# Six modulation pieces in each of seven differential heads instead of eight in each of five

## The reference

```python
def adaln_params(cond, mod_w, mod_b):
    m = jax.nn.silu(cond) @ mod_w + mod_b          # mod_w: (1024, 6144) per layer
    return jnp.split(m[:, None, :], N_MOD, axis=-1)

def layer(x, cond, l, rope, ctx_kv):
    sh_a, sc_a, g_a, sh_f, sc_f, g_f = adaln_params(cond, mod_w[l], mod_b[l])
    o, k, v = token_mixer(modulate(x, norm_attn[l], sh_a, sc_a), l, rope, ctx_kv)
    x = x + g_a * o
    f = conv_ffn(modulate(x, norm_ffn[l], sh_f, sc_f), w_up[l], conv_w[l], conv_b[l], w_down[l])
    return x + g_f * f, k, v
```

## Time and profile before

| | us |
|---|---|
| median of 3 runs (lowest, highest) | 3609.38 (3599.21, 3609.42) |
| the profiled execution's own time | 3618.67 |
| its span, first to last instruction | 3616.9 |
| mean granted TensorE clock | 0.964 |
| TensorE busy | 3342.2 (92%) |
| VectorE, ScalarE, GpSimd busy | 1868.7, 1185.8, 942.6 |
| 40 loads of `wr<-mod_w`, 512 KB each, median to landing | 4.8 |

### The profile page before, as it was taken

The page is one execution under the profiler, slowest core; times in us unless marked ns, Lnnn a source line. Parts: engine busy times, 40 slices in busy tenths (PEclk is TensorE's granted clock), DMA queues, the critical chain, the costliest instruction groups (busy, mean ns, idle before and its releaser), DMA issues. The chain is left out here.

```text
span 3616.9 us, 51583 instructions
## 1 busy us (share of the span) xinstructions
PE 3342.2 (92%) x20797; PEld 3084.3 (85%) x20797; DVE 1868.7 (52%) x2655; ACT 1185.8 (33%) x2106; POOL 942.6 (26%) x726
## 2 busy tenths in 40 slices
PE   5898898998889999999988999999798999999997
PEld 4777777887789999999988777777598999999996
DVE  4555555555155554555545555565416545555454
ACT  3334344444232222122223555555413121222111
POOL 1122112222233322223233121221133322332221
PEclk8999999998899999999999999999899999999998
DMA  6333343113211111111112111101231111111101
GB/s 240 108 107 113 112 125 116 51 40 121 87 42 47 41 53 35 41 37 39 54 38 78 38 30 26 35 23 35 97 99 58 42 36 41 41 37 56 35 29 59
DMA packets 206659, 229.78 MB, mean 64 GB/s; under 512 B 30564, under 2 KB 173533, under 8 KB 205341
## 3 DMA queue, kind: packets, MB, share of 16 engines
q1 hardware_dynamic: 186973, 162.69, 14.8%
q10 hardware_dynamic: 11664, 42.47, 3.5%
q0 software_dynamic: 7856, 22.29, 1.7%
HBM read 181.79 MB, written 31.98 MB: 59 GB/s over the span
## 5 line engine op out<-in xcount | busy, mean ns | idle before, releaser
L205 PE MATMUL psum<-Hh,wh 128*128 128x384 f32 x3360 | 1142.2, 340 | 52.6 <-ACT Hh L377 14.7
L206 PE MATMUL psum<-Hh,wl 128*128 128x384 f32 x3360 | 1131.0, 337 | 0.0
L207 PE MATMUL psum<-Hl,wh 128*128 128x384 f32 x3360 | 1130.9, 337 | 0.0
L286 DVE SCALAR_TENSOR_TENSOR x<-psum,mod,x 128x384 f32<-128x384 f32 (+2 forms) x768 | 377.4, 514 | 684.6 <-PE psum L207 643.2
L205 PEld LDWEIGHTS psum<-Hh,wh 128*128 128x128 f32 x3360 | 636.6, 189 | 63.3 <-issue 35.5
L206 PEld LDWEIGHTS psum<-Hh,wl 128*128 128x128 f32 x3360 | 636.8, 190 | 0.0
L207 PEld LDWEIGHTS psum<-Hl,wh 128*128 128x128 f32 x3360 | 636.5, 189 | 0.0
L816 POOL TENSOR_TENSOR wl<-wr,wh 128x1024 fp32r<-128x1024 f32 x88 | 219.8, 2498 | 986.6 <-ACT wh L735 986.6
L766 ACT ACTIVATE ff_u<-psum 128x768 f32<-128x768 f32 x88 | 71.6, 814 | 1109.2 <-PE psum L207 1109.2
L205 PE MATMUL psum<-ff_ah,ff_dh 128*128 128x384 f32 x1056 | 365.1, 346 | 29.4 <-POOL ff_al L838 20.7
L964 DVE SCALAR_TENSOR_TENSOR ff_c<-ff_u,par,ff_c 128x1153 f32<-128x1153 f32 x176 | 377.4, 2144 | 15.8 <-DVE ff_c L961 5.2
(11 more groups left out here) (217 smaller groups left out, 4267.8 us busy)
## 6 DMA issues: line engine op xcount, KB each, us to landing
wr<-w_up SPq DMA_DIRECT2D x88, 512.0 KB, 3.9
ff_dr<-w_down SPq DMA_DIRECT2D x22, 1024.0 KB, 6.1
da_mw<-mod_w ACTq DMA_DIRECT2D x40, 512.0 KB, 3.9
wr<-mod_w ACTq DMA_DIRECT2D x40, 512.0 KB, 4.8
wr<-w_qkv_diff SPq DMA_DIRECT2D x24, 512.0 KB, 19.2
x<-x_save SPq DMA_DIRECT2D x16, 576.0 KB, 7.5
in_mw<-mod_w SPq DMA_DIRECT2D x8, 1024.0 KB, 12.2
Hh<-oh_save SPq DMA_DIRECT2D x14, 576.0 KB, 9.8
```

What stands on the lines that cost most here:

```text
L205: pe.matmul(out, w_hi, m_hi, start=start, stop=False)
L206: pe.matmul(out, w_lo, m_hi, start=False, stop=False)
L207: return pe.matmul(out, w_hi, m_lo, start=False, stop=stop)
L286: last = dve.scalar_tensor_tensor(g.x[:, m, lo:hi], g.PS[:, bank, lo - n * NB:hi - n * NB], g.mod[:, gate + m, cond:cond + 1], g.x[:, m, l ...
```

## The change

The 40 pieces are numbered through (m = 0 to 39) and put into the list `SLOTS` of (head, step): six in each of heads 0 to 6, at steps 1, 3, 4, 5, 7 and 8, until 40 are placed (heads 0 to 5 have six, head 6 has four, at steps 1, 3, 4 and 5). Slice 1's sum is thus complete after head 1's second piece, and so on. `("MT", i)` stands in front of the piece that begins the next slice, in the same step: head 1 step 4, head 2 step 7, head 4 step 1, head 5 step 4; the last one stands alone in head 6 step 7. TensorE does both at the front of the step, ahead of the scores, and VectorE's bias addition moves to the same place in its order. The request for the next load follows each piece as before. Where the piece before lies in the head before, a wait for the last two uses of that head takes the place of the wait for the piece.

```diff
--- before.py
+++ after.py
@@ -1204,6 +1204,16 @@
         " ck_in cv_in ko_out v_out r_d y_out sub soft y_split wo_in0 wo_in1 wo_hi wo_lo o_in", reused=True)
     free = {WORK: b.free0, WORK + 1: b.free1}
     SLICES = 5
+    SLOTS = [(h, s) for h in range(HEADS - 1) for s in (1, 3, 4, 5, 7, 8)]
+    PIECE = {at: m for m, at in enumerate(SLOTS[:SLICES * KC])}
+
+    def slice_uses(h, s):
+
+        m = SLOTS.index((h, s)) if (h, s) in SLOTS else None
+        if m is None or m > SLICES * KC:
+            return []
+        return [("MT", m // KC - 1)] * (m > 0 and m % KC == 0) + [("M", m)] * (m < SLICES * KC)
+
     mw = [b.mw[:, 0, :], b.mw[:, 1, :]] + [g.wr[:, 1, 4 * j:4 * j + 4, :].rearrange("p k n -> p (k n)") for j in range(2)]
     PROJ = [None, ("k", 1), ("k", 2), ("q", 0), ("q", 1), ("q", 2), ("v", 0), ("v", 1), ("v", 2)]
     PV_AT, ST_AT, BC_AT = {2: [0], 4: [1], 6: [2], 8: [3], 9: [4]}, {3: [0], 5: [1], 7: [2], 9: [3, 4]}, {4: [0], 6: [1], 8: [2], 9: [3, 4]}
@@ -1220,7 +1230,7 @@
         tiles = [("T", s - 1, i) for i in range(len(groups_of(s - 1)))]
         if s == STEPS - 1:
             last = tiles + [("PV", 4), ("ST", 3), ("ST", 4)] + [("W+",)] * ahead2 + [("BC", 3), ("BC", 4)]
-            return [("MT",)] * (h < SLICES) + last
+            return last
         proj = [("W",) + PROJ[s]] if ahead else []
         u = proj + tiles if s == STEPS - 2 else tiles + proj
         u += [("PV", p) for p in PV_AT.get(s, [])]
@@ -1228,7 +1238,7 @@
         if ahead and s in (2, 3):
             u += [("ck",) if s == 2 else ("ko",)]
         u += [("BC", p) for p in BC_AT.get(s, [])]
-        return [("M", s - 1)] * (h < SLICES) + u
+        return slice_uses(h, s) + u
 
     AHEAD = {("W", "k", 0): 0, ("W", "q", 0): 2, ("W", "k", 1): 1, ("W", "q", 1): 3}
     FIRST = [("W", "k", 2), ("ck",), ("ko",), ("W", "q", 2), ("W", "v", 0), ("W", "v", 1), ("W", "v", 2), ("W+",)]
@@ -1397,9 +1407,10 @@
                     copy_out(ring, use, b.ck[:, :], P)
 
             def next_slice(ring, h, s):
-                if ("M", s - 1) in step_uses(h.index, s) and (h.index, s) != (SLICES - 1, STEPS - 2):
-                    act.wait_ge(b.full, ring.done(("M", s - 1)))
-                    load_slice(act, h.index + (s == STEPS - 2), s % KC)
+                m = PIECE.get((h.index, s))
+                if m is not None and m + 1 < len(PIECE):
+                    act.wait_ge(b.full, ring.done(("M", m)))
+                    load_slice(act, (m + 1) // KC, (m + 1) % KC)
 
             def first(ring):
                 load_slice(act, 0, 0)
@@ -1510,15 +1521,18 @@
                 if what == "W+":
                     return project(ring, use, after(h, 2 if ring.head is not None else 1), "k", 0)
                 if what == "M":
-                    k = use[1]
+                    k = use[1] % KC
                     ring.wait_free(pe, free, use)
-                    pe.wait_ge(b.mw_in, 32 * (KC * h.index + k + 1))
+                    pe.wait_ge(b.mw_in, 32 * use[1] + 32)
                     for j in range(4):
                         last = pe.matmul(PS[32 * j:32 * j + 32, bank, :], g.sc[:, k, :], mw[j], start=True, stop=True)
                     last.then_inc(b.full, 1)
                     return
                 if what == "MT":
-                    ring.wait_read(pe, free, ("M", KC - 1))
+                    if ("M", KC * use[1] + KC - 1) in ring.names:
+                        ring.wait_read(pe, free, ("M", KC * use[1] + KC - 1))
+                    else:
+                        ring.wait_earlier_read(pe, free)
                     ring.wait_free(pe, free, use)
                     for k in range(4):
                         last = pe.transpose(PS[:, bank, k * P:(k + 1) * P], b.acc[:, k * P:(k + 1) * P], g.ident[:, :])
@@ -1591,13 +1605,12 @@
             def body(h, ring, ahead, ahead2):
                 for s in range(STEPS):
                     uses = step_uses(h.index, s)
-                    for use in uses[:1]:
-                        if use[0] == "M":
-                            do(ring, h, use)
+                    for use in slice_uses(h.index, s):
+                        do(ring, h, use)
                     if 0 < s < TILES:
                         scores_by_rows(h, s)
                     for use in uses:
-                        if use[0] == "M":
+                        if use[0] in ("M", "MT"):
                             continue
                         if ahead and use == ("PV", 4):
                             scores_by_rows(after(h, 1), 0)
@@ -1652,15 +1665,19 @@
                 dve.scalar_tensor_tensor(b.y[:, (h.odd + p) % 2, 0:n], b.o[:, p % 2, 0:n], b.wsub[:, :], PS[:, ring.bank(use), 0:n],
                                          ALU.mult, ALU.mult).then_inc(free[ring.bank(use)], 1)
 
-            def accumulate(ring, h, k):
-
-                use = ("M", k)
+            def accumulate(ring, use):
+
                 dve.wait_ge(b.full, ring.done(use))
                 src = PS[:, ring.bank(use), :]
-                if k == 0:
+                if use[0] == "MT":
+                    done = add_mod_bias(g, dve, use[1] + 1, src)
+                elif use[1] % KC == 0:
                     done = dve.tensor_copy(b.acc[:, :], src)
                 else:
-                    ring.wait_read(dve, free, ("M", k - 1))
+                    if ("M", use[1] - 1) in ring.names:
+                        ring.wait_read(dve, free, ("M", use[1] - 1))
+                    else:
+                        ring.wait_earlier_read(dve, free)
                     done = dve.tensor_tensor(b.acc[:, :], b.acc[:, :], src, ALU.add)
                 done.then_inc(free[ring.bank(use)], 1)
 
@@ -1676,8 +1693,8 @@
                 for s in range(TILES):
                     for p in BC_AT.get(s - 1, []):
                         normalise(ring, h, p)
-                    if ("M", s - 1) in step_uses(h.index, s):
-                        accumulate(ring, h, s - 1)
+                    for use in slice_uses(h.index, s):
+                        accumulate(ring, use)
                     if s:
                         maxima(h, s)
                     if ahead and s in K_ROPE:
@@ -1690,9 +1707,6 @@
                     combine(h, s)
                     for p in ST_AT.get(s, []):
                         mean_square(ring, p)
-                if h.index < SLICES:
-                    dve.wait_ge(b.full, ring.done(("MT",)))
-                    add_mod_bias(g, dve, h.index + 1, PS[:, ring.bank(("MT",)), :]).then_inc(free[ring.bank(("MT",))], 1)
                 for p in BC_AT[TILES - 1]:
                     normalise(ring, h, p)
                 for p in ST_AT[TILES]:
```

## The result

The changed kernel takes 3579.28 us (median of four runs, 3571.60 to 3582.87), the kernel before 3606.07 us in the same series. The ratio is 0.9925, with a 95% interval of 0.9902 to 0.9949. A second series gave 3579.08 us against 3601.19, ratio 0.9937 (0.9922 to 0.9951). The forecast was 3578; the gain by the medians is 22 to 27 us where 31 was said.

A forecast was written before the change was run, and what follows sets the result against it. TensorE, busy 92%, bounds the kernel; only its idle time and slow stretches can be won. 23.0 + 7.5 + 7.7 - 4.2 - 2.8 = 31.2 us off the 3609.38 us median gives 3578 us, range 3563 to 3597.

The forecast's parts named there:

- Load waits: Heads 0 to 4, steps 2 and 6: TensorE's waits for slice weights go, 23.0 of 26.7 us, 17.67 at step 6.
- Slow clock: Behind step 6's wait, piece and scores return to full clock: 1.5 us in each of five heads, 7.5 us.
- a sign of being wrong: Waits above 1 us at step 4 or 8, ScalarE waiting for weights, or head 2 well above 100 us.
- Pieces back in heads 5 and 6: The ten moved pieces bring new waits, mostly for PSUM banks, in heads 5 and 6: 4.2 us added.
- The transposes: The sum's transposes leave the front of step 9, saving 7.7 us, and cost 2.8 us in the new place.
- Head 0's slow stretch: Head 0 at 220 to 230 us, clock 0.66: left as is; with its slow start about 3 us, either way.
- The cover to watch: Heads 5 and 6: weight loads get slices beside them; landing taken as 18.7 to 19.7 us, tightest with 2 us spare.
- A: Rival: slices stretch weight loads past the 2 us spare, ScalarE stands at the weight conversion; 3581 to 3595 us; 8%.
- C: Rival: loads in steps 3 to 5 and 7 to 8 wait as much as steps 2 and 6 did; 3609 us; 4%.
- D: Rival, slower: weight load beside slice moves to steps 3 or 7, and 13 places pay wait and clock; 3643 us; 3%.
- B: Rival: the wait moves, as another link holds the following step, and half of the 31 us is lost; 3594 us; 6%.

The follow-up runs named there:

- experiment 2: Changed kernel with seven pieces a head, at steps 1, 2, 3, 4, 5, 7, 8 (only step 6 left out); ratio 0.9943 against the kernel before.
- experiment 4: Kernel before, no piece moved, SyncE loading the k weights behind the swap of the queries instead of ahead of it; ratio 0.9947 against the kernel before.
- experiment 6: Changed kernel with the pieces of steps 3 and 7 requested one step ahead instead of two; ratio 0.9938 against the kernel before.
- experiment 5: Changed kernel once more, no edit; ratio 0.9937 against the kernel before.
- experiment 8: Kernel before, eight pieces a head, with request ahead of ScalarE's copies and sum's transposes in front of the next slice; 3573.15 us, ratio 0.9906.
- experiment 3: Changed kernel with seven pieces a head, at steps 1, 3, 4, 5, 6, 7, 8 (only step 2 left out); ratio 0.9980 against the kernel before.

## Why the prediction was right, by its own steps

1. *Load waits (23.0 us of 26.7 to go).* Right: 26.7 - 4.9 = 21.8 us went, with seven waits of 0.44 to 1.55 left where I counted seven summing to 4.2. Right as well that step 6 is the bulk (experiment 2). The reason was half right. More room between request and use does end the waits, but the numbers for it were off: I took the distance from piece to piece, 9 to 13 us before and some 20 after. What counts is the time from ScalarE's issue to the use. Behind a short step it is about 4.2 us before TensorE stands waiting (experiment 4, step 6 of head 2: 4.84 - 0.65), behind a long one 8.5, with two steps 16 to 17. A slice takes 4.8 us in the median, so a short step leaves nothing over. Experiment 6 shows that 8.5 us are enough. What was missing is why step 6 was so much worse than its likes: a weight load issued just ahead of its slice (experiment 4). The prediction had noticed that company and used it only for rivals. In the changed kernel the company is still there (in head 5 the slice requested in step 5 landed after 9.2 us); the piece is just not due before 16.6.

2. *Slow clock (7.5 us).* Right in kind: the clock is 1.00 in heads 1 to 6 of the changed kernel, and likewise in experiment 4, where only the wait was taken away. In size too: between the first trace of before and experiment 4, heads 1 to 4 together became 17.4 us shorter (436.3 to 418.9) and their load waits only 11.0 (20.0 to 9.0); the 6.4 between are 1.6 a head, where 1.5 was said. Two statements failed. The waits left were not all under 1 us: one was 1.55 us at step 8 of head 4, which the prediction had named as a sign of being wrong; it comes with a long issue on ScalarE's queue (below) and cost no slow clock. And in the traces of experiments 5 and 6, waits of 1.60 and 1.72 us at the same place were followed by a slow stretch. With experiment 2, where 2.46 us were not, the runs leave open what besides the wait decides it. Behind the 1.60 us, experiment 5:

```profile
597.76:601.00 3.24, 3.24 (x16) 1.65 (x17) 1.99 (x7) 0.34 (x2) 2.11 (x4) 0.55 0.14 21
```

3. *Pieces back in heads 5 and 6 (4.2 us).* Measured 3.3 us as the cost of spreading, between two kernels without load waits, so 0.49 of the 4.2 could not show there. In head 2 the waits at steps 3 to 5 are those predicted.

4. *The transposes (7.7 out, 2.8 in).* The old place is confirmed (1.55 against 1.54). The new one costs 0.71 instead of 0.56, so the term is 4.2 us, not 4.9.

5. *Head 0's slow stretch* was left as it is, and went: it is absent in the changed kernel and also in the second trace of the kernel before, so it is no effect of the change. Of the 33.2 us, 21.8 of waits, 7.5 to 8 of clock and 4.2 of MT, less 3.3 for the spreading, leave 2.5 to 3. I put them down to this stretch, but that is not shown: head 0 of the second trace of the kernel before has no such stretch and load waits shorter by 2.9 us, and yet is only 1.5 us shorter (115.50 against 117.00).

*The cover to watch was read wrongly.* The prediction says that a weight load takes 18.7 to 19.7 us to land over the whole kernel, beside slices or not the earlier trace rows. These are the times of two loads out of 24, both of the input phase (issued at 10.3 and 11.0 us, L491). For the 22 loads of L1277, all those of the heads among them, the trace has no landing. Asked for L491 alone the view gives the same three numbers, asked for L1277 alone it gives none. The two groups come first below; then a window of 4 us shows the packets of the load issued at 683.12 in head 5, with no slice near. Below them the same for the one issued at 394.68, 1.5 us ahead of a slice, and from experiment 4 a window that begins 4 us after the issue at 392.36 (396.4 to 400.9):

```profile
L1277 SPq DMA_DIRECT2D wr<-w_qkv_diff x22: 378/384/582, 82.3 to 773.7; - x22
L491 SPq DMA_DIRECT2D wr<-w_qkv_diff x2: 681/4629/8577, 10.3 to 11.0; - x2
...
DMA packets 1184, 0.59 MB, mean 147 GB/s; under 512 B 32, under 2 KB 1184, under 8 KB 1184
...
DMA packets 1243, 0.83 MB, mean 208 GB/s; under 512 B 32, under 2 KB 1184, under 8 KB 1243
...
DMA packets 904, 0.95 MB, mean 211 GB/s; under 512 B 37, under 2 KB 767, under 8 KB 903
```

A weight load of 512 KB is 1024 packets of 512 bytes. The first two windows (683.1 to 687.1 and 394.6 to 398.6) hold 1184 - 32 = 1152 of that size, the whole load and the 128 of a key tile: the load was through within 4 us of its issue, with a slice behind it or none. In experiment 4, where load and slice were issued 0.3 us apart, 767 - 37 = 730 of its 1024 packets started more than 4 us after the issue. So "the slice suffers, the weights don't" fits the load at 394.68 of the kernel before, not every order. If the tightest weight load took 4 us as well, it had some 17 us to spare (21.2 less 4), not 2.

Of the rivals, A did not come, and nothing shows its condition, 2 us to spare: no wait of ScalarE for the weights shows in the seven heads of any of the twelve traces. Both its reason (2 us is little) and the one against it (the flat landing time) come from the misreading. By the Trainium skill, DMA: Bandwidth & Descriptors, section "Issuing engines are not separate DMA queues", transfers of different engines interleave on the same 16 DMA engines. The traces agree: for the slice (a wait of 0.65 us alone, 3.60 beside a weight load), and in experiment 4 for the weight load too, as the packets above show. C and D fail on the 4.9 us. B did not come either: the steps behind the removed waits held nothing up, and heads 1 to 5 are as short as was said.

The sum came out well, in part by luck: it holds 23.0 us of waits for 21.8, 4.9 of the transposes for 4.2 and 4.2 of the spreading for 3.3, and it leaves out the head 0 remainder, while the medians gave 22 to 27 us where it says 31. The weak step is the account of why the slices were late. A reader who followed "more room by spreading" would keep the spread pieces; the kernel with the shortest heads keeps eight in a head and asks 3.5 us earlier (experiment 8).

## What to carry to other kernels

Where a single buffer makes a wait, look first at what stands between its release and the next request: here three copies of ScalarE did, and asking ahead of them gained as much as placing the pieces anew. Measure the room from the request to the use, not from use to use. A wait that is long at one step and short at its likes has a cause of its own; list what else is in flight there. When a view gives a landing time, see how many of the loads it counts: here it was two of 24. When a long wait is followed by slower matmuls of the same shape, price it with both.

## What the runs showed of the hardware

- A slice half (512 KB in 4 KB rows) landed 4.8 us after its issue in the median of 40, and 7.7 us after it in head 2 of the kernel before, 1.5 us behind a weight load (512 KB in 512-byte rows). In experiment 3 the same distance made TensorE wait 3.69 us in one head and 0.72 in another.
- In the three traces with six pieces a head and the late request (the changed kernel twice, and experiment 6), ScalarE took 1.37, 1.59 and 2.00 us to issue one DMA (head 4, step 7), against a median of 0.45, and the wait behind it was 1.55 to 1.72 us. Seven more issues of 1.3 to 1.8 us show at other places: step 1 of heads 1 to 3 in experiment 2, step 1 of heads 1 and 3 in experiment 3, step 2 of head 5 in experiment 6, step 3 of head 2 in experiment 8. During each of the ten, a packet was in flight on the DMA queue that the profile calls "instruction"; during the issue of normal length at the same step of head 3 (491.44) there is none. Nothing was run to test whether the packet is the cause. The row in the changed kernel, ScalarE's queue, and the queue in the window 591.59 to 592.96 (packets, MB, share of 16 engines):

```profile
591.59 1.37 ACTq L1257 DMA_DIRECT2D wr<-mod_w  x1
q8 instruction: 1, 0.02, 4.4%
```

- Part of the stretch behind a wait of 1.82 us at step 6 (experiment 3, head 3) ran at the slower clock, 499.88 - 496.75 = 3.13 us for the 18 score matmuls, while behind 1.25 us (head 5) they took 1.87. In experiment 2 the clock was 1.00 behind a wait of 2.46 us at step 2.
